# DeltaNet's Z·V, output and log-decay products from f16 pieces, and attention's exponentials directly behind the transposes

## The chip, the cores and the metric

The kernel runs on 1 core of one Trainium2 chip. The metric is the time of one execution in device microseconds. Five engines work side by side, each through its own program in order: TensorE (PE), VectorE (DVE), ScalarE (ACT), GpSimd (POOL) and SyncE (SP, which here issues loads). They wait for each other on semaphores.

## The reference

One layer of a hybrid encoder over 1024 positions of width 1024: four branches (GLA, RG-LRU, differential attention, DeltaNet) with a gated merge, cross attention over 256 memory positions, and a mixture of 32 experts. The change touches two branches. DeltaNet, in both directions, over chunks of positions:

```python
gam = jnp.cumsum(gc, axis=-1)
decay = jnp.exp(jnp.where(incl, gam[..., :, None] - gam[..., None, :], -jnp.inf))
a_mat = jnp.where(strict, bc[..., None] * kk * decay, 0.0) + jnp.eye(c)
sol = triangular_solve(a_mat, [vc * bc, kc * (bc * jnp.exp(gam))])   # u_val, k_cum
qk = jnp.einsum('bhntd,bhnsd->bhnts', qc, kc) * decay
q_dec = qc * jnp.exp(gam)[..., None]
def step(state, inp):
    v_new = u_i - kc_i @ state
    o = qd_i @ state + qk_i @ v_new
    state = cd_i * state + kd_i.T @ v_new
```

Differential attention, per head and block of 128 queries, with two maps m of 1024 keys each:

```python
s = jnp.einsum('bhmqd,bhmkd->bhmqk', q_blk, kt) + bias[None, :, None]
p = jax.nn.softmax(s, axis=-1)
attn = p[:, :, 0] - lam * p[:, :, 1]
return jnp.einsum('bhqk,bhkd->bhqd', attn, vt)
```

## The kernel before

One list of steps, `plan_schedule`, sets the order of the work up to the experts. Each engine goes through the same list and emits its own part of every step. `dense(..., between=...)` deals out the weight-streaming projections in pieces: a `None` in the list of a branch stands for one such piece (on PE often six f16 products of 512 columns; on ACT and DVE now and then the high and low halves of a weight chunk, L1346 and L1930, or the emptying of a PSUM bank, L1367, L1954 and L1960). For four panels POOL makes the low halves (L2692, L2694). So PE's long f16 projections are woven between the steps of attention and of DeltaNet, and fill its waits.

**Attention** (`diff_*`, 32 units u = head and query block; PE lines 885 to 921). Per unit: `diff_qk` (4 f16 products of 512 columns, L898; DVE adds the bias and takes the minimum, twice, L2249), `diff_exp` (two exponentials of 128x1024 on ACT, L1628), `diff_comb` (DVE: a reciprocal L2259, a factor L2261, the combination of the two maps L2264), `diff_tr` (8 f32 transposes, L911; ACT and DVE empty them as f16 high and low halves, L1637 and L2272), `diff_pv` (24 f16 products of 64 columns, L920; ACT L1644). In the list the unit's transposes are followed by one `None`, then the next unit's exponentials, another `None`, its combination, and this unit's `diff_pv`.

**DeltaNet's first half** (`gdn_a`) makes for each of the eight chunks of 128 positions, in both directions, the decayed matrices L and Q (`NLT`, `NQT`) and writes them to DRAM; the 32x32 diagonal blocks are inverted on DVE (`gdn_inv`, L2361 and L2364, many small rows), the second set of them during the first three chunks of the second half.

**The second half** (`gdn_c`, chunks i = 0 to 7, each for direction d = 0 and 1) has seven parts. A `None` stands behind parts 1 to 5, none behind parts 0 and 6.

- Part 0: POOL spreads the inverted blocks into `NX` and `NZ_` (L2764, 128x512 each, four per chunk) and copies the log decays (`NWK`, L2777), all behind the last chunk's value product. PE makes the sums of log decays (`gbc`, L1006: per direction 2 f32 products of 128 columns) and the first product Y of the block inverse (L1015); ACT the exponential of the sums (`NQD`, L1717).
- Parts 1 to 3: the block inverse Z grows from 32 to 64 to 128 (L1024, L1030, L1015; DVE L2381, L2384, L2385; ACT L1723, L1727).
- Part 4: PE multiplies keys with Z (L1037), ACT empties it (`wk`, L1731), DVE scales Q (L2388).
- Part 5: PE multiplies Z with V (L1043, 4 f32 products of 64 columns per direction, weights `NZ_`, right side `NVT`) and adds wk times the state (L1051); DVE makes V_new (`NVN`, `vn`, L2391).
- Part 6, per direction: PE makes the state's update (L1057), Q times state (L1062) and adds the output product (L1065, 4 f32 products of 64 columns, `NQT` times `NVN`). DVE masks the update (L2396), waits for the output product, and updates the state (L2401, two of 128x128, each with two SBUF operands); from chunk 4 on it adds the output to the other direction's (L2404), before that ACT copies it (L1735).

What an f32 matmul of the program is appears as two instructions in the trace.

The waits around the output product, in PE's part 6 and DVE's:

```python
pe.wait_ge(*v.at("qd", i, d))
...
mm.then_inc(*q.mark("o", i, d))
...
dve.wait_ge(*q.at("o", i, d))
for t in range(2):
    V.scalar_tensor_tensor(NS[d][:, t, :], NS[d][:, t, :], CD[:, d, c, t:t + 1], NKE[d][:, t, :], ALU.mult, ALU.add)
```

## Time and profile before

| | |
|---|---|
| median of 3 runs | 2118.31 us (2117.89 to 2120.36) |
| the profiled execution | 2124.99 us, span of its instructions 2123.2 us |
| PE busy | 1948.5 us (92%), weight loads 1171.6 |
| DVE busy | 1400.9 us (66%) |
| ACT busy | 1096.6 us (52%) |
| POOL busy | 294.1 us (14%) |
| mean granted TensorE clock | 0.96 of full speed |
| HBM | 307.85 MB read, 46.66 MB written |

Busy time counts an engine's instructions on the span from the first to the last. A matmul's own duration contains its way through the array and overlaps with the next one's, so the cost of a group is the distance from its start to the start of the next group. In a row, `[1.13 <-DVE arena L2264]` says that the engine sat idle for 1.13 us before it and was released by DVE's line 2264. `PE` is the matmul, `PEld` the load of its left matrix.

### The profile page before, as it was taken

The page shows a single profiled execution, that of the slowest core. Times are in us where ns is not written, and L with a number is a line of the kernel's source. Part 1 is how long each engine was busy: PE and PEld are TensorE (multiplying, and loading weights), DVE is VectorE, ACT ScalarE, POOL GpSimd, SP SyncE. Part 2 cuts the span into 40 slices and gives each one's busy share as a digit, 9 for nine tenths or more (in the row PEclk, how much of TensorE's full clock was granted, in tenths as well). Part 3 has the DMA queues.
Part 4 walks back from the last instruction along what each step waited for, and adds up shares of the span by engine and source line. Part 5 has one row for each costly group of instructions (what it writes and reads, how often), then busy time and mean ns, then how long its engine had stood idle before and what let it go on. Part 6 is the DMA issues. An engine that isn't in the chain of part 4 may idle for free. (4 is left out here: it accounts for less than half of the span.)

```text
span 2123.2 us, 32456 instructions
## 1 busy us (share of the span) xinstructions
PE 1948.5 (92%) x12820; PEld 1171.6 (55%) x12820; DVE 1400.9 (66%) x1794; ACT 1096.6 (52%) x1590; POOL 294.1 (14%) x276
## 2 busy tenths in 40 slices
PE   5999999899999999999989999898599999999991
PEld 3454566455544546787458865587345444444440
DVE  5555533788855696544442655435789999999985
ACT  3572232666646432212332444334478888888872
POOL 1000200343300613331000000000110111111103
PEclk8999999899999999999999999999699999999996
DMA  5411112112011342321511330311799999999976
GB/s 190 146 53 43 26 40 71 44 48 59 21 37 46 126 162 82 105 70 60 185 55 51 115 99 25 136 56 62 266 351 424 422 422 422 422 422 422 422 321 257
DMA packets 140520, 360.42 MB, mean 170 GB/s; under 512 B 38224, under 2 KB 91632, under 8 KB 113776
## 3 DMA queue, kind: packets, MB, share of 16 engines
q1 hardware_dynamic: 96608, 279.57, 34.9%
q10 hardware_dynamic: 34944, 46.14, 6.2%
q0 software_dynamic: 8848, 33.03, 4.0%
q8 instruction: 85, 1.39, 0.3%
q14 instruction: 35, 0.29, 0.0%
HBM read 307.85 MB, written 46.66 MB: 167 GB/s over the span
## 5 line engine op out<-in xcount | busy, mean ns | idle before, releaser
L780 PE MATMUL psum<-arena 128*128 128x512 f16 (+2 forms) x6000 | 1020.5, 328 | 12.9 <-ACT arena L1367 5.5
L780 PEld LDWEIGHTS psum<-arena 128*128 128x128 f16 x6000 | 571.4, 99 | 400.7 <-issue 30.9
L1184 PE MATMUL psum<-arena 128*128 128x512 f16 x2304 | 515.3, 383 | 15.5 <-issue 12.4
L739 DVE SCALAR_TENSOR_TENSOR arena<-arena 128x2048 f16<-128x2048 f32 x192 | 437.3, 2286 | 60.4 <-ACT arena L733 60.1
L733 ACT ACTIVATE arena<-arena 128x2048 f16<-128x2048 f32 x192 | 365.3, 1908 | 71.1 <-DMA arena<-in_w_dram 42.5
L1184 PEld LDWEIGHTS psum<-arena 128*128 128x128 f16 x2304 | 225.3, 99 | 283.5 <-issue 26.8
L1930 DVE SCALAR_TENSOR_TENSOR arena<-arena 128x512 f16<-128x512 f32 (+1 forms) x193 | 130.0, 694 | 129.5 <-ACT arena L1346 129.1
L2804 POOL DMA_INDIRECT arena<-xhat,arena x32 | 67.2, 2100 | 855.3 <-PE psum L1173 452.0
L1346 ACT ACTIVATE arena<-arena 128x512 f16<-128x512 f32 (+1 forms) x212 | 127.0, 616 | 27.1 <-DMA arena<-in_xattn_wo_dram 5.8
L1367 ACT ACTIVATE arena<-psum,arena 128x512 f32<-128x512 f32 x64 | 43.9, 685 | 160.5 <-PE psum L780 155.0
L1431 ACT ACTIVATE arena<-psum 128x512 f32<-128x512 f32 (+3 forms) x51 | 29.9, 586 | 126.1 <-PE psum L780 126.1
L1954 DVE SCALAR_TENSOR_TENSOR arena<-arena,psum 128x512 f32<-128x512 f32 x64 | 43.8, 684 | 61.3 <-PE psum L780 40.7
L1395 ACT ACTIVATE arena<-arena 128x256 f32<-128x256 f32 x64 | 26.7, 417 | 106.8 <-DVE arena L1966 105.8
L2249 DVE CUSTOM_DVE_ANT_0 arena<-psum,arena 128x1024 f32<-128x1024 f32 x64 | 75.6, 1219 | 0.6 <-PE psum L898 0.5
L1628 ACT ACTIVATE arena<-arena 128x1024 f32<-128x1024 f32 x64 | 72.9, 1145 | 4.5 <-DVE arena L2249 4.5
L1984 DVE SCALAR_TENSOR_TENSOR arena<-psum,arena 128x512 f16<-128x512 f32 x36 | 24.8, 690 | 68.0 <-ACT arena L1431 39.1
L1637 ACT ACTIVATE arena<-psum 128x512 f16<-128x512 f32 x64 | 34.8, 594 | 58.2 <-PE psum L911 36.8
L1966 DVE SCALAR_TENSOR_TENSOR arena<-psum,arena 128x512 f32<-128x512 f32 x32 | 22.1, 690 | 62.7 <-PE psum L780 62.7
L2764 POOL TENSOR_TENSOR arena<-arena 128x512 f32<-128x512 f32 x32 | 35.0, 1114 | 144.4 <-DMA arena<-gdn_inv 90.5
L2692 POOL TENSOR_SCALAR arena<-arena 128x512 f32<-128x512 f32 x19 | 36.5, 1920 | 132.0 <-ACT arena L1346 132.0
L797 PE MATMUL psum<-arena 128*128 128x128 f32 x144 | 23.0, 315 | 28.0 <-DVE arena L2054 28.0
L1845 ACT ACTIVATE arena<-psum 128x512 f32<-128x512 f32 x64 | 38.1, 597 | 12.7 <-PE psum L1184 12.4
(381 smaller groups left out, 2179.3 us busy)
## 6 DMA issues: line engine op xcount, KB each, us to landing
arena<-in_w_dram SPq DMA_DIRECT2D x192, 1024.0 KB, 11.9
arena<-in_merge_w_dram SPq DMA_DIRECT2D x64, 256.0 KB, 3.1
yrows<-arena ACTq DMA_DIRECT2D x32, 512.0 KB, 7.7
arena<-in_w_in_dram SPq DMA_DIRECT2D x48, 256.0 KB, 2.8
gdn_lq<-arena ACTq DMA_DIRECT2D x8, 1024.0 KB, 4.0
arena<-gdn_lq ACTq DMA_DIRECT2D x8, 1024.0 KB, 5.1
arena<-in_xattn_wkv_dram SPq DMA_DIRECT2D x32, 256.0 KB, 3.0
yrows<-arena POOLq DMA_DIRECT2D x1, 7680.0 KB, 24.2
```

The lines of the kernel that those rows point to most:

```text
L733: nc.scalar.activation(half_of(pieces(e, m)[0], half), half_of(XLAND[m], half), ACT.Copy, scale=WS).then_inc(w_hi[m], 1)
L739: nc.vector.scalar_tensor_tensor(half_of(lo, half), half_of(XLAND[m], half), WS, half_of(hi, half), ALU.mult, ALU.subtract).then_inc(w_lo[ ...
L780: mm = nc.tensor.matmul(bank[prt[0]:prt[1], c0:c1], lhs[a](k), rhs[b](k), start=(k == 0 and a + b == 0), stop=(k == nk - 1 and a == 1))
L1184: mm = nc.tensor.matmul(PS[:, bank, :], left[a][:, k, :], right[b][:, k, columns], start=k + a + b == 0, stop=(k == n - 1 and a == 1))
L1346: S.activation(W[i % 2][0][:, 2 * j:2 * j + 2, 0:wide], LAND[c % NLAND][:, :, 0:wide], ACT.Copy, scale=WS).then_inc(*act_hi.mark(c))
L1367: S.activation(SG[gate_no[n] % 2], bank, ACT.Tanh, scale=0.5 / WS, bias=half_b[:, 8 * kind[1] + kind[2]:8 * kind[1] + kind[2] + 1]).then_i ...
L1628: S.activation(DS[u % 2][:, m, :], DS[u % 2][:, m, :], ACT.Exp, scale=-1.0, bias=d_mx[u % 2][:, m:m + 1], accum_out=d_l[u % 2][:, m:m + 1])\
L1845: S.activation(YB[s][:, half, :], PS[:, 5 + half, :], ACT.Copy, scale=1 / (WS * GSCALE)).then_inc(act_y, 1)
L1930: V.scalar_tensor_tensor(W[i % 2][1][:, 2 * j:2 * j + 2, 0:wide], LAND[c % NLAND][:, :, 0:wide], WS, W[i % 2][0][:, 2 * j:2 * j + 2, 0:wid ...
L1954: V.scalar_tensor_tensor(dst, gate, 1.0, bank, ALU.add, ALU.mult).then_inc(*e.mark(n))
L2249: V.tensor_tensor_reduce(out=DS[u % 2][:, m, :], in0=PS[:, 2 + 2 * m:4 + 2 * m, :].rearrange("p a b -> p (a b)"), in1=DWH[:, 896 - P * qt: ...
L2804: G.indirect_dma_start(XR[e % 2], None, XH_D, bass.IndirectOffsetOnAxis(IDX[:, e:e + 1], 0)).then_inc(rows_in[e % 2], 16)
```

## The change

1. **Attention.** In the list of steps `diff_exp(u + 1)` moves ahead of the `None` that stood between it and the transposes.
2. **Z times V.** V is kept as two f16 pieces (`NVT16`: ACT writes the high one instead of `NVT`, DVE subtracts the low one, four operations of 128x512 each). Z gets two f16 pieces per direction and chunk: in part 3 ACT copies the high one (`z_hi`), DVE subtracts the low one (`z_lo`). The product becomes high·high, high·low and low·high: 12 f16 products instead of 4 f32 ones.
3. **The output product.** Q's pieces (`NQT16`, over `NY`) are made in part 4, the high one by ACT, the low one by POOL, behind its operations of part 1. V_new's pieces (`NVN16`, over `NWK`) are made by ACT in part 5 and by DVE at the head of each direction's part 6. Again 12 f16 products per direction instead of 4 f32 ones.
4. **The sums of log decays.** The log decays are scaled by 32 once, held from below at -60000 and split into two f16 pieces (3 small DVE operations in `gdn_gam`); POOL copies both for each direction and chunk (`NWK16`, over `NVN16`'s place), now behind all four spreads, and waits for the last chunk's output product. PE's sums (4 f16 products of 128 columns per direction) stand behind both directions' Y of part 0; ACT's exponential takes the scale back out.

The orders that result, as the builder lays them out. Lines of the changed kernel are shifted: L2396 became L2439 and L2401 became L2444, L2437 is V_new's low piece, L2426 Z's.

DVE in part 6 of chunk 3 and the head of part 0 of chunk 4, before:

```order
L2391 TENSOR_TENSOR arena<-psum,arena 128x256 x2
L2396 TENSOR_TENSOR arena<-psum,arena 128x256
L2401 SCALAR_TENSOR_TENSOR arena<-arena 128x128 x2
L2396 TENSOR_TENSOR arena<-psum,arena 128x256
L2401 SCALAR_TENSOR_TENSOR arena<-arena 128x128 x2
L2381 TENSOR_TENSOR arena<-psum,arena 128x512 x2
```

and now:

```order
L2432 TENSOR_TENSOR arena<-psum,arena 128x256 x2
L2437 TENSOR_TENSOR arena<-arena 128x256
L2439 TENSOR_TENSOR arena<-psum,arena 128x256
L2444 SCALAR_TENSOR_TENSOR arena<-arena 128x128 x2
L2437 TENSOR_TENSOR arena<-arena 128x256
L2439 TENSOR_TENSOR arena<-psum,arena 128x256
L2444 SCALAR_TENSOR_TENSOR arena<-arena 128x128 x2
L2419 TENSOR_TENSOR arena<-psum,arena 128x512 x2
```

A low piece stands ahead of each direction's masked update, the second one behind the first direction's state updates.

PE from part 6 of a chunk to part 1 of the next, before:

```order
L1057 MATMUL psum<-arena 128x128 x2
L1062 MATMUL psum<-arena 128x128 x2
L1065 MATMUL psum<-arena 128x64 x4
L1006 MATMUL psum<-arena 128x128 x2
L1015 MATMUL psum<-arena 128x128 x4
L1006 MATMUL psum<-arena 128x128 x2
L1015 MATMUL psum<-arena 128x128 x4
L1024 MATMUL psum<-arena 128x128 x4
```

and now (L1074 the output, L1019 is Y, L1083 the decay sums, L1028 the first product of part 1):

```order
L1063 MATMUL psum<-arena 128x128 x2
L1068 MATMUL psum<-arena 128x128 x2
L1074 MATMUL psum<-arena 128x64 x12
L1019 MATMUL psum<-arena 128x128 x8
L1083 MATMUL psum<-arena 128x128 x8
L1028 MATMUL psum<-arena 128x128 x4
```

The decay sums moved from ahead of each Y to behind both.

ACT in attention, before (L1637 empties transposes, L1346 is a weight chunk's high half, L1628 the exponentials):

```order
L1644 ACTIVATE arena<-psum,arena 128x64
L1637 ACTIVATE arena<-psum 128x512 x2
L1346 ACTIVATE arena<-arena 128x512
L1628 ACTIVATE arena<-arena 128x1024 x2
L1644 ACTIVATE arena<-psum,arena 128x64
```

and now, at the same place:

```order
L1660 ACTIVATE arena<-psum,arena 128x64
L1653 ACTIVATE arena<-psum 128x512 x2
L1644 ACTIVATE arena<-arena 128x1024 x2
L1362 ACTIVATE arena<-arena 128x512
L1660 ACTIVATE arena<-psum,arena 128x64
```

The weight copy moved behind the exponentials; this is so in 8 of the 31 units, and the others' order is as before.

The diff:

```diff
@@ plan_schedule
-        diff += [("diff_qk", u + 1)] * more + [("diff_tr", u, 0), ("diff_tr", u, 1), None] + [("diff_exp", u + 1)] * more
+        diff += [("diff_qk", u + 1)] * more + [("diff_tr", u, 0), ("diff_tr", u, 1)] + [("diff_exp", u + 1)] * more + [None]
@@ tiles
+        NVT16 = [f16(BR + 6144 + 1024 * x, TT, 256) for x in range(2)]
+        NZ16 = [[f16(UN + 2048 + 1536 * d + 256 * x, NH, P) for x in range(2)] for d in range(2)]
+        NQT16 = [[f16(UN + 2560 + 1536 * d + 256 * x, NH, P) for x in range(2)] for d in range(2)]
+        NVN16 = [[f16(UN + 5120 + 1280 * d + 512 + 128 * x, 2, P) for x in range(2)] for d in range(2)]
+        NWK16 = [[f16(UN + 5120 + 1280 * d + 512 + 128 * x, 2, P) for x in range(2)] for d in range(2)]
...
@@ PE, gdn_c
-                            pe.wait_ge(*po.at("lab", i, d))
-                            for t in range(2):
-                                mm = nc.tensor.matmul(B1[:, t, :], NWK[d][:, t, :], inc_b if d else inc_f, start=True, stop=True)
-                            mm.then_inc(*q.mark("gbc", i, d))
...
                         elif part == 5:
+                            pe.wait_ge(*v.at("z_lo", i, d))
                             for h in range(NH):
-                                nc.tensor.matmul(PS[:, 3 + 3 * d, h * 64:h * 64 + 64], NZ_[d][:, SLOT_OF[h], :],
-                                                 NVT[:, c, h * 64:h * 64 + 64], start=h == 0, stop=False)
+                                for x, y in ((0, 0), (0, 1), (1, 0)):
+                                    nc.tensor.matmul(PS[:, 3 + 3 * d, h * 64:h * 64 + 64], NZ16[d][x][:, SLOT_OF[h], :],
+                                                     NVT16[y][:, c, h * 64:h * 64 + 64], start=h + x + y == 0, stop=False)
...
+                            pe.wait_ge(*po.at("qt_lo", i, d))
+                            pe.wait_ge(*v.at("vn_lo", i, d))
                             for h in range(NH):
-                                mm = nc.tensor.matmul(PS[:, 2 + 3 * d, h * 64:h * 64 + 64], NQT[s][d][:, SLOT_OF[h], :],
-                                                      NVN[d].rearrange("p t n -> p (t n)")[:, h * 64:h * 64 + 64],
-                                                      start=False, stop=h == NH - 1)
+                                for x, y in ((0, 0), (0, 1), (1, 0)):
+                                    mm = nc.tensor.matmul(PS[:, 2 + 3 * d, h * 64:h * 64 + 64], NQT16[d][x][:, SLOT_OF[h], :],
+                                                          NVN16[d][y].rearrange("p t n -> p (t n)")[:, h * 64:h * 64 + 64],
+                                                          start=False, stop=h == NH - 1 and x == 1)
                             mm.then_inc(*q.mark("o", i, d))
+                    for d in range(2 if part == 0 else 0):
+                        B1 = PS[:, 3 + 3 * d, :].rearrange("p (h n) -> p h n", h=NH)
+                        pe.wait_ge(*po.at("lab", i, d))
+                        for t in range(2):
+                            for x in range(2):
+                                mm = nc.tensor.matmul(B1[:, t, :], NWK16[d][x][:, t, :], INC16[d], start=x == 0, stop=x == 1)
+                        mm.then_inc(*q.mark("gbc", i, d))
@@ ACT, gdn_c
+                        elif part == 5:
+                            act.wait_ge(*v.at("vn", i, d))
+                            S.activation(NVN16[d][0], NVN[d], ACT.Copy).then_inc(*a.mark("vn_hi", i, d))
...
+                    for d in range(2 if part in (3, 4) else 0):
+                        if part == 3:
+                            act.wait_ge(*a.at("z", i, d, 6))
+                            S.activation(NZ16[d][0], NZ_[d], ACT.Copy).then_inc(*a.mark("z_hi", i, d))
+                        else:
+                            act.wait_ge(lq_in[s], 48 * (i // 2) + 48)
+                            S.activation(NQT16[d][0], NQT[s][d], ACT.Copy).then_inc(*a.mark("qt_hi", i, d))
@@ DVE, gdn_c
+                        elif part == 3:
+                            dve.wait_ge(*a.at("z_hi", i, d))
+                            V.tensor_tensor(NZ16[d][1], NZ_[d], NZ16[d][0], ALU.subtract).then_inc(*v.mark("z_lo", i, d))
...
                         elif part == 6:
+                            dve.wait_ge(*a.at("vn_hi", i, d))
+                            V.tensor_tensor(NVN16[d][1], NVN[d], NVN16[d][0], ALU.subtract).then_inc(*v.mark("vn_lo", i, d))
                             dve.wait_ge(*q.at("u", i, d))
@@ POOL, gdn_c
                             spread(NX[d], d, d).then_inc(*po.mark("x", i, d))
                             spread(NZ_[d], 1 - d, d).then_inc(*po.mark("z", i, d))
+                        for d in range(2):
+                            if i:
+                                pool.wait_ge(*q.at("o", i - 1, d))
...
-                            G.tensor_copy(NWK[d].rearrange("p t (u n) -> p (t u) n", u=2), heads(LAd[:, d, c_, :]))\
-                                .then_inc(*po.mark("lab", i, d))
+                            for x in range(2):
+                                G.tensor_copy(NWK16[d][x].rearrange("p t (u n) -> p (t u) n", u=2), heads(LA16[x][:, d, c_, :]))\
+                                    .then_inc(*po.mark(*(("lab", i, d) if x else ("lab_hi", i, d))))
...
+                    elif part == 4:
+                        for d in range(2):
+                            pool.wait_ge(*counter("act_gdn").at("qt_hi", i, d))
+                            G.tensor_tensor(NQT16[d][1], NQT[s][d], NQT16[d][0], ALU.subtract).then_inc(*po.mark("qt_lo", i, d))
```

## Rows read from the trace of the kernel before

**Rows 1.** The page: busy time of each engine, and the longest chain by engine.

```profile
PE 1948.5 (92%) x12820; PEld 1171.6 (55%) x12820; DVE 1400.9 (66%) x1794; ACT 1096.6 (52%) x1590; POOL 294.1 (14%) x276
...
PE 25%; DVE 2%; DMA 1%; issue 1%; POOL 0%; ACT 0%; POOLq 0%; DVEq 0%
```

**Rows 2.** Stretches: length; PE, PEld, DVE, ACT, POOL busy; clock, DMA, GB/s.

```profile
372.00:600.00 228.00, 206.87 (x1710) 115.77 (x1709) 190.66 (x318) 145.49 (x272) 79.17 (x58) 0.97 0.15 40
...
809.00:995.00 186.00, 179.67 (x1532) 144.17 (x1531) 101.62 (x213) 39.14 (x91) 56.63 (x77) 1.00 0.25 73
```

**Rows 3.** Timeline, chunks 4 to 5: start us, duration, engine, line.

```profile
922.40 1.00 PE L1065 MATMUL psum<-arena 128*128 128x64 f32 x8
923.25 0.66 PE L1057 MATMUL psum<-arena 128*128 128x128 f32 x4
...
925.03 0.66 PE L1006 MATMUL psum<-arena 128*128 128x128 f32 x4
925.53 1.06 PE L1015 MATMUL psum<-arena 128*128 128x128 f32 x8
...
925.73 0.39 ACT L1717 ACTIVATE arena<-psum 128x256 f32<-128x256 f32 x1 [6.20 <-PE psum L1006]
```

**Rows 4.** Timeline of PE, attention: the f16 products of 64 columns.

```profile
479.81 0.87 PE L920 MATMUL psum<-arena 128*128 128x64 f16 x24 [0.41 <-DVE arena L2272]
480.52 1.03 PE L898 MATMUL psum<-arena 128*128 128x512 f16 x4
```

**Rows 5.** Timeline, attention: a unit whose weight copy precedes the exponentials.

```profile
439.92 0.63 ACT L1346 ACTIVATE arena<-arena 128x512 f16<-128x512 f32 x1
440.44 1.15 ACT L1628 ACTIVATE arena<-arena 128x1024 f32<-128x1024 f32 x1
...
444.76 1.09 PE L911 MATMUL psum<-arena 128*128 128x128 f32 x8 [1.13 <-DVE arena L2264]
```

**Rows 6.** Timeline, attention: another such unit, on PE.

```profile
423.74 1.03 PE L898 MATMUL psum<-arena 128*128 128x512 f16 x4
...
424.73 1.09 PE L911 MATMUL psum<-arena 128*128 128x128 f32 x8
```

**Rows 7.** Timeline, part 6 of chunk 6: POOL and DVE.

```profile
968.55 0.40 POOL L2777 COPY arena<-arena 128x256 f32<-128x256 f32 x1
968.70 0.66 PE L1057 MATMUL psum<-arena 128*128 128x128 f32 x4
968.91 2.09 POOL L2764 TENSOR_TENSOR arena<-arena 128x512 f32<-128x512 f32 x2
968.98 2.16 DVE L2401 SCALAR_TENSOR_TENSOR arena<-arena 128x128 f32<-128x128 f32 x2 [0.94 <-PE psum L1065]
```

**Rows 8.** Groups by shape, 809 to 995 us: busy us, mean ns; idle before.

```profile
L2764 POOL TENSOR_TENSOR arena<-arena 128x512 f32<-128x512 f32 x30 | 32.5, 1104 | 100.6 <-PE psum L1051 53.9 <-DMA arena<-gdn_inv 46.6
...
L1346 ACT ACTIVATE arena<-arena 128x512 f16<-128x512 f32 x9 | 5.6, 624 | 0.5 <-ACT arena L1367 0.5
...
L1960 DVE TENSOR_TENSOR arena<-arena 128x512 f32<-128x512 f32 x2 | 1.4, 692 | 0.1
```

**Rows 9.** Timeline, chunks 0 and 1.

```profile
822.90 0.38 ACT L1731 ACTIVATE arena<-psum 128x256 f32<-128x256 f32 x1 [1.56 <-PE psum L1037]
...
827.42 0.76 DVE L2391 TENSOR_TENSOR arena<-psum,arena 128x256 f32<-128x256 f32 x2
828.10 0.42 DVE L2361 TENSOR_TENSOR arena<-arena 128x210 f32<-128x210 f32 x1
...
830.18 1.11 DVE L2364 TENSOR_TENSOR arena<-arena 128x220 f32<-128x220 f32 x1
...
831.96 0.66 PE L1006 MATMUL psum<-arena 128*128 128x128 f32 x4
...
832.72 0.61 DVE L2401 SCALAR_TENSOR_TENSOR arena<-arena 128x128 f32<-128x128 f32 x2
...
853.69 0.71 PE L1057 MATMUL psum<-arena 128*128 128x128 f32 x4 [2.12 <-DVE arena L2391]
```

More of the change, by code:

```diff
@@ L434, in build @@
         LRUP = scol(256)
+        INC16 = [LRUP[:, 64 * d:64 * d + 64].bitcast(F16) for d in range(2)]
         g_em, g_ee, g_eem, g_mid, g_end = (scol(TT) for _ in range(5))
@@ L488, in build @@
         n_las, n_bes = n_t[2], n_t[3]
+        NVT16 = [f16(BR + 6144 + 1024 * x, TT, 256) for x in range(2)]
+        NZ16 = [[f16(UN + 2048 + 1536 * d + 256 * x, NH, P) for x in range(2)] for d in range(2)]
+        NQT16 = [[f16(UN + 2560 + 1536 * d + 256 * x, NH, P) for x in range(2)] for d in range(2)]
+        NVN16 = [[f16(UN + 5120 + 1280 * d + 512 + 128 * x, 2, P) for x in range(2)] for d in range(2)]
+        LA_SCALE = 32.0
+        LA16 = [n_t[1].bitcast(F16)[:, 64 * x:64 * x + 64].rearrange("p (d c h) -> p d c h", d=2, c=TT) for x in range(2)]
+        NWK16 = [[f16(UN + 5120 + 1280 * d + 512 + 128 * x, 2, P) for x in range(2)] for d in range(2)]
         LAS = n_las.rearrange("p (d c h) -> p d c h", d=2, c=TT)
@@ L1709, in _ @@
                     i, part = step[1:]
+                    s = i % 2
                     a, v, q = (counter(f"{e}_gdn") for e in ("act", "vec", "pe"))
@@ L2297, in _ @@
                         V.tensor_tensor(dst, dst, NSQ, ALU.mult).then_inc(*v.mark("norm", s))
+                elif step == ("gdn_tm", "nv"):
+                    v, a = counter("vec_gdnp"), counter("act_gdnp")
+                    for j in range(4):
+                        dve.wait_ge(*a.at("tm", "nv", j))
+                        V.tensor_tensor(NVT16[1][:, 2 * j:2 * j + 2, :], PS[:, 2 + j, :].rearrange("p (c n) -> p c n", c=2),
+                                        NVT16[0][:, 2 * j:2 * j + 2, :], ALU.subtract).then_inc(*v.mark("tm_lo", j))
                 elif what == "gdn_scal":
@@ L2326, in _ @@
                                 .then_inc(*v.mark("slots", by_slot is n_bes, u))
+                    V.tensor_scalar(n_tmp[:, 0:64], n_la, LA_SCALE, -60000.0, ALU.mult, ALU.max).then_inc(*v.mark("la_scaled"))
+                    dve.wait_ge(*v.last())
+                    V.tensor_copy(n_t[1].bitcast(F16)[:, 0:64], n_tmp[:, 0:64]).then_inc(*v.mark("la_hi"))
+                    dve.wait_ge(*v.last())
+                    V.tensor_tensor(n_t[1].bitcast(F16)[:, 64:128], n_tmp[:, 0:64], n_t[1].bitcast(F16)[:, 0:64], ALU.subtract).then_inc(*v.mark("la_lo"))
                     for par in range(2):
@@ L2788, in _ @@
                                 .then_inc(*po.mark("kd", i, d))
+                    elif part == 4:
+                        for d in range(2):
+                            pool.wait_ge(*counter("act_gdn").at("qt_hi", i, d))
+                            G.tensor_tensor(NQT16[d][1], NQT[s][d], NQT16[d][0], ALU.subtract).then_inc(*po.mark("qt_lo", i, d))
                 elif what == "experts_first":
```

7 lines of the change are left out of this document (4 added, 3 removed).

## The prediction

> **What bounds the kernel now.** I read the page's busy times and its longest chain first: TensorE (PE) is busy for 1948.5 us of the 2123.2, and the last stretch of the program belongs to PE too, in lines that the change leaves alone [rows 1]. So what counts is how long PE needs for the two stages that are edited, and I read those by the table of stretches [rows 2]. In attention (372 to 600 us) PE is busy for 206.9 of 228 us and VectorE (DVE) for 190.7: two engines that take turns in waiting for each other. In DeltaNet's second half, the eight `gdn_c` chunks from 809 to 995 us, PE is busy for 179.7 of 186 us. Only 6.3 us of PE stalls are left there, DVE has 84 us free, GpSimd (POOL) 129. PE's program is in order and nothing after 995 us starts by a clock of its own, so a microsecond won or lost by PE in either stage is one at the end.
>
> **What PE saves in a chunk.** The cost of a group of matmuls is the distance between the starts of neighbouring groups. The four f32 products of the output in one direction take 923.25 - 922.40 = 0.85 us, the four of Z and V, of the same shape and number, as much; the two sums of log decays 925.53 - 925.03 = 0.50 and, behind other f32 groups, 0.45 [rows 3]. Their f16 form has three products for one, of 64 columns each. Attention has exactly this form: 24 of them take 480.52 - 479.81 = 0.71 us, 0.030 each [rows 4]. So twelve take 0.36. A 128-column f16 product is taken as two of these, so the four of a decay sum take 0.23. Saved in both directions: 0.98 + 0.98 + 0.49 = 2.45 us in a chunk, 19.6 us in eight.
>
> This rests on a row of f32. The Trainium skill says otherwise: FP8 and Floating Point Precision, section TensorE Precision Notes, has a true f32 product as four passes through the array. With 64 columns at 2.4 GHz that is an estimate of 0.107 us for a product, not 0.21, and the sum of savings would be some 5 us instead of 19.6; the group of four in the trace contradicts it.
>
> **What the chunk pays for that.** The pieces are made by three engines, and where they stand in each queue decides.
>
> 1. *Decay sums.* They now stand behind both Y products of part 0, and behind them comes a product that waits for ACT's exponential. Both Y groups take 1.78, the sums 0.46. The first exponential can start 0.20 behind its sum and takes 0.39 [rows 3], plus 0.1 to wake PE: PE, ready at 2.24 us of the chunk, starts at 2.70. This is a new stall of 0.45 us, 3.6 in all; the start of the chunk is as late as before, and the sums' saving is nearly all given back.
>
> 2. *Z's pieces.* Two ACT copies of 0.62 and two DVE subtractions of 0.69 (a 128x512 tile on either engine) [rows 8] lie between part 3 and part 5, where PE has two dense pieces and the wk products, some 3.7 us of cover. I cost them at nothing in quiet chunks; DVE is not quiet in chunks 0 and 1 (below). The DVE halves of `NVT16` (four of 0.69) follow ACT's copies one by one before DeltaNet's first stage, where POOL's first product is awaited anyway: nothing. The three small operations on log decays: nothing, they are needed 90 us later.
>
> 3. *Q's pieces.* ACT copies 128x512 twice behind its wk copies, POOL subtracts twice, 1.10 each by its spreads of the same size [rows 8]. In a chunk let V be the moment at which the first direction's value product ends. POOL's second subtraction ends about V+1.25, and only then do its four spreads of the next chunk run, 1.04 each, to V+5.4. Before, they began at V+0.25.
>
> 4. *The output product of the second direction.* This is the place that decides. On DVE the order is now: low piece of V_new, masked update, the two state updates, for one direction and then for the other. The state update waits for that direction's output product. So the second low piece stands behind the first direction's output, and PE's second output behind that low piece. PE ends output 0 at V+3.4 and could start output 1 at V+4.35. DVE begins the state updates 0.28 later than output 0 ended, as in the trace (968.70 to 968.98). Undisturbed they take 0.61 for two, and the low piece about 0.4, half of the 0.76 of two such tiles [rows 9]: ready at V+4.8, a stall of 0.5, and 0.9 in chunks 4 to 7, where DVE's addition of `NO` (0.41) stands between. This is the lower bound.
> But POOL is not idle then. At 968.91 POOL runs two spreads, and DVE's two state updates, which read two SBUF tiles each, take 2.16 us instead of 0.61 [rows 7, 9]: each waited for one POOL operation to end. With POOL busy to V+5.4, then with the two decay copies of 0.40, the updates end at V+5.6, the low piece at V+6.25: a stall of 2.0, and 2.35 in chunks 4 to 6. I take the upper values, since the spreads cover exactly this stretch by the rows.
>
> 5. *The output of the first direction.* Its low piece of V_new is in time unless a weight chunk's low half (L1930) stands ahead of it: chunks 2 and 4. There both meet POOL's spreads, and I count 1.3 more for each.
>
> 6. *Chunks 0 and 1.* Here DVE also works on the second block inverse (L2361, L2364: small operations on two SBUF tiles). One of them took 1.11 with POOL at work, about 0.43 alone. Before, V_new was made at 827.42 and output 1 ended at 831.96, where the next chunk's first group starts. ACT's two wk copies of 0.38 began at 822.90; they begin 0.5 earlier now, and Q's first copy of 0.62 ends behind them at 823.8 [rows 8, 9]. DVE's own work on two tiles lets POOL begin with Q's low pieces at about 824.15. POOL then runs six operations, with one DVE operation let in after each, every 1.15 us: to 831.05. DVE's last two rows, V_new and six more rows end at 835.3, and only then comes the low piece, at 835.7. PE's output 0 ends at 836.2, output 1 at 838.15: chunk 0 ends 6.2 us later, its savings included. In chunk 1 V_new was late already, and PE waited 2.12 for it at 853.69. Z's subtractions (1.4), Q's (each holds DVE up by about 0.7) and the products of V_new behind them make it 2.5 later still.
>
> Chunk by chunk, savings (2.0 with the stall of point 1) against stalls: +6.2, +2.5, +1.3, 0.0, +1.7, +0.4, -0.5 (it had 0.9 of stall before), and -1.1 in the last, which has no spreads behind it. **The stage: +10.5 us.**
>
> **Attention.** The exponentials move ahead of one dense piece. PE's and DVE's orders don't change; on ACT a weight copy (L1346) stood between transposes and exponentials in 8 of 31 units and now stands behind. It held up the exponential by 440.44 - 439.92 = 0.52 us. PE then waited 1.13 for DVE's combination, which waits for the exponential [rows 5]: three units are like this, and each gives back the 0.52, some more with the next wait. In four the scores of the next unit start at 423.74 and the transposes at 424.73, only 0.13 more than those scores take [rows 6]: 0.13 each. The eighth gives nothing. 1.6 + 0.5, rounded up for the waits behind: **-2.5 us.** POOL's halves of these weights come 2.3 us later and aren't due before the panel's last quarter.
>
> **Sum.** +10.5 - 2.5 = +8.0 us on the profiled execution, whose own time is 2124.99 (span 2123.2). The median of the runs shown is 2118.3, 6.7 lower; I add the same change to it: 2126.3.
>
> **Rivals.** About 0.2%, 4.2 us, is what a measurement of this kernel can tell from no change.
> - *The savings win.* If POOL's spreads don't coincide with the state updates, point 4 costs its lower bound, 4 x 0.5 + 4 x 0.9 = 5.6; chunk 0 keeps only the six rows ahead of the low piece, 3 more; of 19.6 - 3.6 = 16.0 us remain 7.4, with attention 9.9: 2108.4. For it: POOL has 129 us free, and some state updates in the trace took 0.61. Against it: Q's subtractions push the spreads later, onto the updates.
> - *A wash.* Half of the contention: the stage ends midway between +10.5 and -7.4, at +1.5, attention at -2.5: 2117.3.
> - *Attention turns slower.* One mechanism: POOL's scaling of the moved weight copy becomes ready within 0.1 us of DVE's combination. If POOL starts first, DVE waits up to the length of that operation, some 1.4 us, in seven units, 0.85 net each: +6 in place of -2.5, so 2134.8. It decides from a delay of 0.1 us in DVE.
> - *The f16 products are no faster behind f32 groups.* Then nothing is saved and the stalls stay: 2126.3 + 19.6 = 2145.9. Against it: [rows 4] is the same form, with a new left matrix for each product too.
>
> **Chances.** Forecast (2120 to 2133) 0.48; the savings win 0.22; a wash 0.18; attention slower 0.09; no saving 0.03. The range, short of the far ends: 2108 to 2135, from the savings' win to attention's loss. Faster by over 0.2%: 0.23; within: 0.22; slower: 0.55.
>
> **What would show it.** Right: PE waits before the output product, released by DVE's low piece, about 2 us in most chunks, and before the Z·X product by ACT's exponential, 0.45; state updates of 1.1 us each; stage 809 to 995 about 196 us; attention about 225.5. Wrong: PE stalls before the output of 0.5 to 0.9 with state updates of 0.36 us, or chunk 0 no longer than before; then the stage is under 180 us and the kernel faster.

## The result, and the profile after

The changed kernel takes 2142.23 us (median of 4 runs, 2139.90 to 2142.92) against 2118.10 before (4 runs): a ratio of 1.0111, 95% interval 1.0098 to 1.0123. The forecast was 2126.3, with 2135 as its upper end. The direction was right, the size three times too small.

The page's busy times, where [rows 1] stood before:

```profile
PE 1938.2 (91%) x12948; PEld 1162.4 (54%) x12948; DVE 1435.2 (67%) x1833; ACT 1118.2 (52%) x1638; POOL 328.8 (15%) x310
```

TensorE (PE) works 10 us less in a longer execution. The stretches that answer to [rows 2], attention and DeltaNet's second half (length; PE, PEld, DVE, ACT, POOL busy; clock, DMA, GB/s):

```profile
372.00:600.00 228.00, 208.97 (x1736) 118.19 (x1735) 192.06 (x326) 149.66 (x280) 87.85 (x62) 0.98 0.16 43
802.00:1014.10 212.10, 176.24 (x1651) 136.40 (x1650) 132.53 (x242) 61.40 (x139) 83.04 (x109) 0.91 0.22 64
```

The second half takes 212.0 us (802.11 to 1014.07), 184.7 before (809.36 to 994.04): +27.3. The clock column fell from 1.00 to 0.91. Chunk by chunk, from the first product of a chunk (before the decay sums L1006, now Y, L1019) to that of the next:

| chunk | 0 | 1 | 2 | 3 | 4 | 5 | 6 | 7 | sum |
|---|---|---|---|---|---|---|---|---|---|
| before, us | 22.60 | 25.35 | 23.51 | 22.11 | 22.10 | 22.38 | 24.17 | 22.46 | 184.7 |
| after | 29.75 | 30.23 | 31.19 | 22.46 | 23.49 | 26.62 | 25.28 | 22.94 | 212.0 |
| difference | +7.2 | +4.9 | +7.7 | +0.4 | +1.4 | +4.2 | +1.1 | +0.5 | +27.3 |
| forecast | +6.2 | +2.5 | +1.3 | 0.0 | +1.7 | +0.4 | -0.5 | -1.1 | +10.5 |
| PE waits, before | 0.3 | 2.7 | 1.3 | 0.0 | 0.0 | 0.0 | 0.9 | 0.9 | 6.1 |
| PE waits, after | 6.8 | 7.5 | 8.0 | 2.2 | 2.8 | 3.4 | 3.7 | 1.1 | 35.5 |

PE's waits in this stage (us in total, times, longest; L1063 is the state's update, L1074 the output product, L1041 keys times Z, L1028 the first product of part 1; L2432 makes V_new, L2437 its low piece):

```profile
PE psum L1063 <- DVE arena L2432: 18.6, 3, 7.2
PE psum L1074 <- DVE arena L2437: 11.7, 8, 2.7
PE psum L1041 <- ACT arena L1744: 2.1, 2, 1.2
PE psum L1028 <- DVE arena L2419: 2.0, 6, 0.3
```

Chunk 1, in order of time. L2426 is Z's low piece, L1987 and L1957 belong to the woven projections, L2429 scales Q, L2399 and L2402 are rows of the second block inverse, L2841 Q's low piece, L2809 the spreads:

```profile
845.25 1.29 DVE L2426 TENSOR_TENSOR arena<-arena 128x512 f16<-128x512 f32 x2 [0.24 <-ACT arena L1759]
...
846.95 2.72 POOL L2841 TENSOR_TENSOR arena<-arena 128x512 f16<-128x512 f32 x2 [11.70 <-ACT arena L1762]
...
847.18 1.47 DVE L1987 TENSOR_TENSOR arena<-arena 128x512 f32<-128x512 f32 x1
...
848.42 1.46 PE L788 MATMUL psum<-arena 128*128 128x512 f16 x6
848.57 2.55 DVE L2429 TENSOR_TENSOR arena<-arena 128x256 f32<-128x256 f32 x2
849.62 4.99 POOL L2809 TENSOR_TENSOR arena<-arena 128x512 f32<-128x512 f32 x4
851.05 1.52 DVE L1957 SCALAR_TENSOR_TENSOR arena<-arena 128x512 f16<-128x512 f32 x1
852.49 1.23 DVE L2399 TENSOR_TENSOR arena<-arena 128x228 f32<-128x228 f32 x1
...
853.75 1.12 DVE L2402 TENSOR_TENSOR arena<-arena 128x228 f32<-128x228 f32 x1
...
856.57 0.76 DVE L2432 TENSOR_TENSOR arena<-psum,arena 128x256 f32<-128x256 f32 x2
...
857.05 1.23 PE L1063 MATMUL psum<-arena 128*128 128x128 f32 x4 [7.17 <-DVE arena L2432]
...
858.92 0.85 PE L1074 MATMUL psum<-arena 128*128 128x64 f16 x12
```

From 846.95 to 854.61 GpSimd (POOL) works without a pause, and each VectorE (DVE) operation on two SBUF tiles takes about as long as one of POOL's: L2429 2.55 for two instead of 0.75, L2399 1.23 where one after 854.61 takes 0.39. The value products end at 848.4, PE has one dense piece, and V_new is made at 856.57. The Trainium skill has this rule (SBUF — State Buffer, section Who interferes with whom): a DVE instruction with two SBUF inputs contends with a GpSimd instruction that reads SBUF. The durations above agree.

What follows the wait is the part that the forecast lacks. PE's update of the state (L1063) takes 1.23 where it took 0.71 behind a wait in [rows 9], and the output's twelve products reach from 858.92 to 859.58, where the next group starts: 0.66 instead of the 0.35 of chunk 3. The clock over the same time:

```profile
848.00:852.00 4.00, 1.88 (x12) 0.90 (x10) 4.00 (x4) 0.00 (x0) 4.00 (x5) 1.00 0.01 1
852.00:856.00 4.00, 0.00 (x0) 0.00 (x0) 3.86 (x6) 0.00 (x0) 2.62 (x3) 0.55 0.25 66
856.00:860.00 4.00, 2.95 (x22) 2.89 (x23) 2.22 (x7) 0.94 (x3) 0.17 (x1) 0.50 0.02 4
860.00:862.00 2.00, 2.00 (x19) 1.94 (x19) 1.44 (x4) 0.19 (x1) 0.63 (x2) 0.50 0.00 0
862.00:864.00 2.00, 2.00 (x21) 2.00 (x19) 1.37 (x3) 0.38 (x1) 1.66 (x4) 0.84 0.00 0
864.00:866.00 2.00, 1.66 (x19) 1.50 (x18) 0.91 (x2) 0.66 (x2) 1.46 (x3) 1.00 0.00 0
```

It fell to 0.50, its 1.2 GHz level, while PE waited, and came back at 863. In slices of 2 us over the stage, PE's busy time times (1 - clock) comes to 13.7 us; this is called lost pace here. It lies behind the waits of chunks 0, 1 and 2, and again at 937 to 945, 965 to 969 and 992 to 996. Before, the same sum is 0.0. The stage alone, before and now:

```profile
809.36:994.04 184.68, 178.35 (x1522) 143.08 (x1521) 100.93 (x210) 39.14 (x91) 56.27 (x77) 1.00 0.25 74
```

```profile
802.11:1014.07 211.96, 176.10 (x1650) 136.28 (x1649) 132.53 (x242) 61.40 (x139) 82.93 (x109) 0.91 0.22 64
```

PE's busy time without its lost pace fell from 178.35 to 176.10 - 13.7 = 162.4, by 16.0. So the sum closes: 29.4 us more of waiting and 13.7 of lost pace, less 16.0 saved, are +27.1, of +27.3 measured.

### The profile page after: what moved, and what is told of

Read it like the earlier page. It is cut to its first block and busy times, and to the rows that moved or that the text cites. A ratio compares the mean times of both kernels' runs of the same rounds, so it can differ in the third digit from the quotient of the medians.

```text
span 2140.3 us, 32849 instructions
## 1 busy us (share of the span) xinstructions
PE 1938.2 (91%) x12948; PEld 1162.4 (54%) x12948; DVE 1435.2 (67%) x1833; ACT 1118.2 (52%) x1638; POOL 328.8 (15%) x310
## 5 line engine op out<-in xcount | busy, mean ns | idle before, releaser
L1957 DVE SCALAR_TENSOR_TENSOR arena<-arena 128x512 f16<-128x512 f32 (+1 forms) x193 | 131.0, 700 | 115.0 <-ACT arena L1362 114.7
L2735 POOL TENSOR_SCALAR arena<-arena 128x512 f32<-128x512 f32 x19 | 44.7, 2352 | 133.8 <-ACT arena L1362 133.8
L805 PE MATMUL psum<-arena 128*128 128x128 f32 x144 | 23.2, 316 | 28.4 <-DVE arena L2081 28.4
L919 PE MATMUL psum<-arena 128*128 128x128 f32 x256 | 35.0, 281 | 9.9 <-DVE arena L2291 9.8
```

Source lines behind the costliest of these rows:

```text
L1957: V.scalar_tensor_tensor(W[i % 2][1][:, 2 * j:2 * j + 2, 0:wide], LAND[c % NLAND][:, :, 0:wide], WS, W[i % 2][0][:, 2 * j:2 * j + 2, 0:wid ...
L2735: G.tensor_scalar(landed_c, landed_c, WS, None, ALU.mult).then_inc(*counter("pool_w_scaled").mark(c))
```

## The experiments

Ratios are to the kernel before, run on the same chip, with 95% intervals.

**1. Attention alone.** Edit: the kernel before with the list's line of the change.

> The kernel before with the attention edit alone. The recorded theory gives it 2.5 us: 2115.6 us against 2118.1, a ratio of 0.9988. The rival reads the trace of the changed kernel, in which DeltaNet's second half begins at 802.1 us instead of 809.4: if all of that comes from the edit, 2111 us, a ratio of 0.9965, and attention (372 to 600 us) has its last value product near 580 us instead of 584.5.

Measured: 2113.89 against 2116.61 us, 0.9991 (0.9978 to 1.0004). The interval holds 1, so the times alone show no gain; the traces do. Attention's value products run from 391.6 to 584.3 us, from 392.3 to 587.9 before: 2.9 us shorter; and in all traces of this case they span 192.7 to 193.1 us with the edit and 195.6 to 196.6 without it. The forecast's 2.5 holds. Of the 7.3 us by which the changed kernel's trace was ahead at 802, 2.6 lie there, 2.0 ahead of attention and 2.7 behind it. The latter two are no effect of the edit: the stretch behind attention took 221.5 us before and 218.4 in experiment 12, by the same code.

**2. DeltaNet alone.** Edit: the changed kernel with the list's old line.

> The changed kernel with attention's old order, so the DeltaNet edits alone. DeltaNet's second half took 212.0 us in the changed kernel and 184.7 before. If this whole difference is its own, the time is 2118.1 + 27.3 = 2145.4 us (ratio 1.0129), and the sum with the attention edit gives the changed kernel back. Rival: the second half's length depends on where attention leaves the other engines, and then the stage is shorter than 205 us here.

Measured: 2144.76 us, 1.0133 (1.0116 to 1.0150), the stage 210.4 us. The loss is the DeltaNet edits' own.

**3. Q's low pieces on DVE.**

```diff
-                            G.tensor_tensor(NQT16[d][1], NQT[s][d], NQT16[d][0], ALU.subtract).then_inc(*po.mark("qt_lo", i, d))
+                        V.tensor_tensor(NQT16[d][1], NQT[i % 2][d], NQT16[d][0], ALU.subtract).then_inc(*v.mark("qt_lo", i, d))
```

> The changed kernel with Q's low pieces on VectorE (behind its scaling of Q in part 4) instead of GpSimd. Theory: GpSimd's two subtractions and the four spreads pushed behind them are what VectorE's inverse rows wait for in chunks 0 to 2; TensorE's waits for V_new fall from 18.6 us to 6 or less, its clock no longer halves there, the output product's waits fall from 11.7 to about 5: 2116 to 2122 us. Rival: the spreads meet the rows wherever they start, as they did before, and VectorE has 1.4 us more to do in each chunk: the waits for V_new stay above 12 us and the time above 2134.

Measured: 2138.79 us, 1.0104 (1.0088 to 1.0121). PE's waits:

```profile
PE psum L1063 <- DVE arena L2432: 17.4, 4, 6.8
PE psum L1074 <- DVE arena L2437: 10.3, 8, 2.4
```

The rival was right. In chunk 1 DVE now carries the subtractions itself, 2.97 us for two since the spreads begin with them, at 848.42, and V_new's wait there is 6.8 instead of 7.2 us.

**4. Without the inverse's rows.** Edit: the loop over the rows of the second block is left out, its last three operations stay; so the second block isn't inverted.

> The changed kernel without the rows of the second block inverse (that part of the computation is left out). Theory: the excess of chunks 0 to 2 (7.1 + 4.9 + 7.7 us against before) is these rows meeting GpSimd, with the halved clock that follows; it goes, less 1 us: 2142.2 - 18.7 = 2123.5 us, no wait for V_new over 1 us, and the clock halves in chunks 4 to 6 alone. Rival: V_new is late since its pieces and Z's stand ahead of it on VectorE and ScalarE; then waits for V_new stay, and the time is above 2136.

Measured: 2128.66 us, 1.0050 (1.0034 to 1.0067); the stage 196.2 us instead of 212.0. Chunk 0 is at 22.7, chunk 1 at 25.1, as before the change; chunk 2 is at 27.6, where it was 23.5 before. The time lies between theory and rival: the rows account for 13.6 us by the medians, not for all 18.7. PE still waits 4.6 us for V_new and 14.2 for its low pieces.

**5. Z times V alone.** Edit: the kernel before with part 2 of the change only.

> The kernel before with Z times V from f16 pieces alone: no pieces of Q or V_new, decay sums as before, attention as before. A group of twelve f16 products stands 0.35 us from the next one in the changed kernel's trace, four f32 ones 0.85, so TensorE saves 16 x 0.5 = 8.0 us. Theory: VectorE's two more subtractions (1.3 us) delay V_new in chunks 0 to 2 only, by some 1.3 us each where it was already late: 2118.1 - 8.0 + 4 = 2114, stage about 180.5 us (184.7 before), the clock at full level throughout. Rival: these subtractions alone push V_new behind GpSimd's spreads and bring the waits of 5 to 7 us and the halved clock: above 2130.

Measured: 2125.82 us, 1.0029 (1.0015 to 1.0043), between theory and rival; the stage takes 193.3 us, 6.8 of them lost pace. PE's waits for V_new:

```profile
PE psum L1061 <- DVE arena L2407: 11.0, 3, 5.5
```

Chunks 3 to 7 are 21.2 to 22.9 us long, 0.3 to 1.3 less each than before: there the pieces of Z are hidden and the products' saving arrives. In chunk 1, V_new is 5.5 us late instead of 2.1: by an estimate from both traces 1.3 for Z's low pieces, 1.0 since PE gets there sooner, 0.9 since one more DVE operation falls under the spreads. So neither Q's pieces nor V_new's are needed for the long wait.

**6. The rows dealt out otherwise.**

```diff
-            if i < 3 and part in (1, 2, 4) or (i, part) == (0, 5):
+            if i < 3 and part in (1, 2, 3) or (i, part) == (3, 0):
```

> The changed kernel with the second block inverse's rows dealt out otherwise: behind parts 1, 2 and 3 of chunks 0 to 2 and part 0 of chunk 3, instead of parts 1, 2 and 4 and once part 5. So none of them stands between V_new's operands and V_new. Theory: the waits for V_new (18.6 us) fall under 4 us, since rows meet GpSimd's subtractions and spreads only where they stand in part 4; the halved clock of chunks 0 to 2 (9.5 us of lost pace) goes with them: 2142.2 - 15 - 9 = 2118 us. Rival: VectorE has too much work in these chunks wherever it stands: 2132 or more.

Measured: 2138.45 us, 1.0083 (1.0060 to 1.0106), waits for V_new 16.5 us. The theory fell, by a fault of the edit's: a row behind part 3 still stands ahead of V_new in DVE's queue. In chunk 1 five of these six operations took 1.12 to 1.36 us under POOL's work.

**7. V_new's low pieces in part 5.**

```diff
-                            V.tensor_tensor(NVN16[d][1], NVN[d], NVN16[d][0], ALU.subtract).then_inc(*v.mark("vn_lo", i, d))
+                    for d in range(2 if part == 5 else 0):
+                        dve.wait_ge(*a.at("vn_hi", i, d))
+                        V.tensor_tensor(NVN16[d][1], NVN[d], NVN16[d][0], ALU.subtract).then_inc(*v.mark("vn_lo", i, d))
```

> The changed kernel with V_new's two low pieces on VectorE in part 5, directly behind V_new, instead of at the head of each direction's part 6; nothing else is moved. Theory: TensorE's waits for the low pieces (11.7 us in 8) fall to 3 or less, and the halved clock in chunks 4 to 6 (some 5 us of lost pace) goes: 2142.2 - 8.7 - 5 = 2128.5 us, chunks 0 to 2 unchanged. Rival: the state updates behind GpSimd's spreads hold TensorE anyway, through the masked update or the next chunk's value product: less than 4 us gained, above 2138.

Measured: 2132.84 us, 1.0059 (1.0042 to 1.0076), 9.4 us better than the change and 4.3 short of the theory. The 11.7 us of waits for low pieces are gone; 6.4 came back ahead of the next chunk's Y (L1019), for DVE's addition of `NO` behind the state updates (L2445):

```profile
PE psum L1063 <- DVE arena L2432: 18.5, 3, 7.2
PE psum L1019 <- DVE arena L2445: 6.4, 6, 2.1
```

**8. Both.**

> The last two edits together: rows dealt out otherwise and V_new's low pieces in part 5. If the two waits and the clock behind them are the whole loss, the gains add up: 2118 - 13.7 = 2104 us, faster than the kernel before by 0.6%, stage about 173 us. Rival: one wait takes the other's place: 2115 or more.

Measured: 2129.80 us, 1.0047 (1.0034 to 1.0060). The rival's time was right, its reason in part: V_new's waits, 16.5 us, had not gone at all, and `NO`'s addition brings 6.4 as in experiment 7.

**9. The inverse begun earlier, low pieces in part 5.** Edit: the second set of diagonal blocks is read behind the first inverse, twelve rows stand ahead of chunk 0, none behind parts 3 and 4.

> The changed kernel with V_new's low pieces in part 5 and the second block inverse begun earlier: its diagonal blocks are read right behind the first inverse, its first twelve rows stand in the dense pieces ahead of chunk 0, the others behind parts 1 and 2 of chunks 0 to 2, none behind part 4. Theory: with rows out of the stretch in which GpSimd works, V_new is in time; against the kernel with both edits (2129.8) its waits for V_new of 16.5 us fall under 3 and 5.6 us of lost pace go with them: 2129.8 - 13.5 - 5 = 2111 us. Rival: VectorE is behind in these chunks for another reason than rows: above 2122.

Measured: 2122.10 us, 1.0019 (1.0009 to 1.0029), at the rival's bound. But the rows were the reason for most of it: V_new's waits fell from 16.5 to 4.6 us. PE waited 2.6 us ahead of the stage, and ran at half the clock there too: the diagonal blocks landed late (DVE waits 3.13 us for them, to 795.41), and the rows met POOL's first spreads at 798.15.

**10. The same rows, with Z times V and attention alone.**

> The kernel before with Z times V from f16 pieces, the attention edit, and the second block inverse begun earlier as in the last kernel. From the run with Z times V alone (2125.8): its waits for V_new were 11.0 us and its lost pace 6.8; without them 2108, with attention's 2 us 2106: faster than before by 0.5%. Rival: rows behind parts 1 and 2 hold Z's low piece and the waits move there: 2116 or more.

Measured: 2113.66 us, 0.9972 (0.9962 to 0.9983), between theory and rival. Within the stage the clock stays full. Ahead of it PE waited 2.9 us, and the clock halved there too.

**11 and 12. A wait by itself.** Edit: the kernel before, with 10 or 5 idle operations ahead of V_new in chunks 4 to 7.

```diff
+                            if i >= 4 and d == 0:
+                                dve.wait_ge(inv_out[1], 32)
+                                for k in range(10):
+                                    V.tensor_scalar(NU[1], NU[1], 1.0, None, ALU.mult).then_inc(*v.mark("delay", i, k))
+                                    dve.wait_ge(*v.last())
```

> The kernel before with ten idle operations of some 0.7 us on VectorE ahead of the first direction's V_new in chunks 4 to 7 (no part of the change). TensorE stalls some 5.4 us in each. Theory: after such a stall the granted clock halves for 5 to 6 us, as in chunks 0 to 2 of the changed kernel, and each costs some 3 us beyond its stall: 2118 + 4 x 8.4 = 2152. Rival: the halved clock belongs to the f16 products or to the time at which they run, not to a stall: 2118 + 21.6 = 2140, clock at full level between 809 and 1015.

> The same with five such operations: TensorE stalls 1.8 us in each of the four chunks. If the halving needs a long stall, as chunk 3 of the changed kernel (1.9 us, no halving) lets one think, 2118 + 7 = 2125 and full clock; if stalls of this size are enough, as after 1.8 + 0.65 us in its chunk 4, up to 2118 + 7 + 12 = 2137.

Measured: 2160.19 us, 1.0196 (1.0179 to 1.0213), and 2138.87, 1.0095 (1.0077 to 1.0113). The waits came out longer than expected, the cost behind them as the first theory has it. With ten, PE waits 8.2, 8.2, 8.2 and 5.2 us, and the four chunks are 39.9 us longer; 10.2 of that is no waiting. Chunk 4, by the table of stretches:

```profile
922.00:930.00 8.00, 0.87 (x4) 0.87 (x5) 7.76 (x10) 0.00 (x0) 3.88 (x4) 0.60 0.00 0
930.00:934.00 4.00, 4.00 (x21) 4.00 (x21) 1.52 (x6) 0.00 (x0) 0.39 (x1) 0.51 0.21 66
936.00:938.00 2.00, 2.00 (x21) 2.00 (x20) 0.98 (x3) 0.47 (x2) 1.15 (x2) 1.00 0.00 0
```

With five, waits of 3.7, 3.7 and 3.0 us are each followed by the halved clock, one of 1.5 is not; what 1.8 us in each chunk would do, the waits being twice that, these chunks don't tell. The program around them is the kernel before: the halving needs no f16 product and no pieces. Chunk 1, which holds no idle operation, shows more (the last line is from the table of stretches):

```profile
850.82 1.22 PE L1057 MATMUL psum<-arena 128*128 128x128 f32 x4 [2.12 <-DVE arena L2396]
...
852.68 1.81 PE L1065 MATMUL psum<-arena 128*128 128x64 f32 x8
...
852.00:856.00 4.00, 4.00 (x21) 4.00 (x20) 1.46 (x4) 0.38 (x1) 0.70 (x2) 0.50 0.02 4
```

It is the wait of 2.12 us of [rows 9]. There L1057 took 0.71 behind it; here 1.22, and the chunk 28.6 us instead of 25.35, with 2.7 us of waits in both. So this short wait cost its length in three executions and 3 us more in a fourth. The Trainium skill says that an idle gap can lower PE's clock, so that the next work starts at half (TensorE: Matmul & The Clock Gate, section HAM oscillation — how this bites in real kernels); these runs agree.

**13 to 15. Control and the two better versions.** Edit of all three; 14 adds Z times V and attention, 15 is the whole change with V_new's low pieces in part 5:

```diff
+        ... + [("gdn_read", 1)] * (p == 8)
-    gdn += [("gdn_back", 0)] + [None] * 6 + [("gdn_load_inv", 0), ("gdn_load_inv", 1), ("gdn_read", 1)] + [None] * 7
+    gdn += [("gdn_back", 0)] + inv(1, 0) + [None] * 2 + inv(1, 1) + [None] * 2 + inv(1, 2) + [None] * 2
+    gdn += [("gdn_load_inv", 0), ("gdn_load_inv", 1)] + [None] * 7
-            if i < 3 and part in (1, 2, 4) or (i, part) == (0, 5):
-                gdn += inv(1, 3 * i + (i > 0) + (1, 2, 4, 5).index(part))
+            if i < 3 and part in (1, 2):
+                gdn += inv(1, 2 * i + part + 2) + inv(1, 9) * ((i, part) == (2, 2))
```

> The kernel before with nothing but the second block inverse begun earlier (nine rows ahead of chunk 0, none behind part 4). It is the control for the next two. Before, V_new was late by 2.1 us in chunk 1, with 0.6 behind it: theory, that goes and nothing else: 2118.7 - 2.7 = 2116, ratio 0.9987. Rival: its rows ahead of chunk 0 meet GpSimd's first spreads, and it is 2120 or more.

> As the kernel with Z times V, the attention edit and the inverse begun earlier (2113.7), but the diagonal blocks are read before the first inverse is ready, so that the rows ahead of chunk 0 run from 792 to 799 us and not from 799 to 813. There TensorE waited 2.9 us ahead of the stage and ran at half the clock for 2 to 4 us. Theory: 5 us less, 2108.5, ratio to before 0.995. If the Z-times-V pieces win nothing beyond the control, it is the control's time less attention's 2 us: 2114.

> The whole change with V_new's low pieces in part 5 and the inverse begun earlier in the same way. From its predecessor (2122.1), whose trace shows 2.6 us of wait ahead of the stage and 4.5 us of lost pace within: 2115, ratio 0.998. If the whole change is sound and only its place was wrong, it beats the control; if the f16 output product doesn't pay for its pieces, it stays behind the kernel with Z times V alone by 5 us or more.

Measured:

| | us | ratio to before | stage, us | clock |
|---|---|---|---|---|
| 13, rows moved alone | 2114.05 | 0.9975 (0.9964 to 0.9987) | 181.3 | 1.00 |
| 14, with Z times V and attention | 2107.85 | 0.9962 (0.9947 to 0.9976) | 175.5 | 1.00 |
| 15, the whole change | 2114.95 | 0.9983 (0.9972 to 0.9994) | 186.3 | 0.97 |

The stage's row in 13, 14 and 15:

```profile
807.50:988.80 181.30, 177.80 (x1522) 143.09 (x1522) 92.14 (x192) 39.15 (x91) 53.87 (x76) 1.00 0.25 75
```

```profile
804.50:980.10 175.60, 171.14 (x1587) 134.83 (x1586) 104.87 (x208) 47.59 (x107) 55.10 (x76) 1.00 0.26 78
```

```profile
805.40:991.80 186.40, 168.23 (x1650) 128.58 (x1650) 124.50 (x224) 61.60 (x139) 84.13 (x108) 0.97 0.24 73
```

Kernel 14 has the lowest median of all, and beats both kernels of this case. Chunk 1 in it:

```profile
840.18 1.29 DVE L2402 TENSOR_TENSOR arena<-arena 128x512 f16<-128x512 f32 x2 [0.36 <-ACT arena L1743]
...
841.95 0.69 PE L1056 MATMUL psum<-arena 128*128 128x128 f32 x4
...
843.36 2.60 POOL L2781 TENSOR_TENSOR arena<-arena 128x512 f32<-128x512 f32 x2 [14.23 <-DMA arena<-gdn_inv]
843.38 0.69 DVE L1938 SCALAR_TENSOR_TENSOR arena<-arena 128x512 f16<-128x512 f32 x1
843.99 0.75 DVE L2408 TENSOR_TENSOR arena<-psum,arena 128x256 f32<-128x256 f32 x2
...
844.64 0.61 PE L1062 MATMUL psum<-arena 128*128 128x128 f32 x4
```

V_new (L2408) is made at 843.99, with nothing but a weight's low half (L1938) between it and the spreads' start at 843.36; PE goes on at 844.64 with no wait. The control tells how much of it is due to the rows alone: 4.3 us by the medians, with 3.4 us off the stage. Z times V takes 5.8 us more off the stage; the medians of 13 and 14 are 6.2 apart, which holds the attention edit's 2 to 3 us too.

Kernel 15 beats the kernel before, but not by the change: the control, with the rows alone, is as fast (2114.05 by 2114.95, though 15 has the attention edit as well). Its stage is 10.8 us longer than 14's, and 5.0 longer than the control's. What it waits for (L1020 is Y, L1064 the state's update, L1029 part 1; L2446 adds `NO`, L2433 makes V_new, L2420 masks Y):

```profile
PE psum L1020 <- DVE arena L2446: 6.4, 6, 2.1
PE psum L1064 <- DVE arena L2433: 4.9, 3, 3.1
PE psum L1029 <- DVE arena L2420: 2.6, 4, 1.5
```

PE is busy for 2.9 us less than in 14, and 4.7 of its busy time is lost pace; its waits are 17.6 us, 4.2 in 14. So the f16 output product and decay sums together cost more than their faster matmuls give, with the pieces where 15 makes them. The two were not run apart, so what each of them costs is not shown.

## Why the prediction was right or wrong

Forecast: +8.0 us. Measured: +24.1. By the prediction's own steps:

- **What PE saves in a chunk** (2.45 us). Twelve f16 products: 912.38 - 912.03 = 0.35 against the 0.36 taken; right, and the four-pass estimate of 0.107 us for an f32 product stays contradicted. The eight products of the decay sums start 0.056 apart at full clock, 0.45 in all against 0.46; both Y take 1.87, not 1.78. By distances of starts that is 2.4 a chunk, some 19.3 in all against 19.6. PE's busy time fell by only 16.0. An estimate of why: where a wait follows, the last product's way through the array is no longer covered by the next one and counts as busy, as in the 0.61 us that the row of the sums lasts.
- **Point 1**, a new wait of 0.45 behind the sums: 0.34, in six chunks. Right. The view names DVE's L2419 as the releaser; but the mask that this product needs was done at 895.18 in chunk 3, and ACT's exponential at 895.99, 0.15 before PE went on, as forecast.
- **Point 2**, Z's pieces for nothing: right in chunks 3 to 7, wrong before (experiment 5).
- **Points 3 and 4.** Chunk 3 went nearly as written, with V, the end of the first value product, at 908.97:

```profile
907.93 2.42 POOL L2841 TENSOR_TENSOR arena<-arena 128x512 f16<-128x512 f32 x2 [11.27 <-ACT arena L1762]
...
910.30 4.26 POOL L2809 TENSOR_TENSOR arena<-arena 128x512 f32<-128x512 f32 x4
...
911.14 0.61 PE L1063 MATMUL psum<-arena 128*128 128x128 f32 x4
...
912.65 2.06 DVE L2444 SCALAR_TENSOR_TENSOR arena<-arena 128x128 f32<-128x128 f32 x2 [0.44 <-PE psum L1074]
...
914.63 0.61 DVE L2437 TENSOR_TENSOR arena<-arena 128x256 f16<-128x256 f32 x1
...
915.39 0.51 PE L1074 MATMUL psum<-arena 128*128 128x64 f16 x12 [1.88 <-DVE arena L2437]
```

  The spreads run from V+1.3 to V+5.6 (forecast 1.25 and 5.4), the state updates take 2.06 for two (forecast 2.16), and PE waits 1.88 before output 1 (2.0). Later chunks show 2.7 and 2.5 (2.35); 0.65 in chunk 4, where output 0 had taken the wait. Chunk 2 has none of this wait, since V_new came after the spreads there. Right but for that.
- **Point 5**, 1.3 us at output 0 in chunks 2 and 4: 1.82 in chunk 4, 0.38 in chunk 2, where V_new was the later one. Half right.
- **Point 6.** Right for chunks 0 and 1 in place and size: +7.2 and +4.9, which are +4.7 and +2.1 without the lost pace, against 6.2 and 2.5. It stopped one chunk too early. The last rows of the inverse stand behind part 4 of chunk 2 as well, with two operations of 1.03 and 0.69 us behind them:

```profile
885.38 1.03 DVE L2405 TENSOR_SCALAR arena<-arena 128x1024 f32<-128x1024 f32 x1
...
887.71 1.22 PE L1063 MATMUL psum<-arena 128*128 128x128 f32 x4 [6.06 <-DVE arena L2432]
```

  Six operations of the rows, of 0.93 to 1.20 us (0.2 alone), ran under POOL's, V_new came at 887.26, and PE waited 6.1. Forecast: +1.3, measured: +7.7, or +5.1 without the lost pace. This step failed.
- **"Savings against stalls"**, the sum itself. It priced a wait at its length. The forecast's waits were 30.1 us (10.5 + 19.6), the measured ones 29.4 more than before: that total was right, partly by errors that cancel. The 13.7 us of lost pace behind them had no term: the clock stood at 1.00 in this stage before [rows 2], and the forecast took it to stay there. They make most of the 16 us that were missing. This is the step that decided, and experiments 11 and 12 show it on a kernel without the change.
- **Attention**, -2.5: 2.9 us in the trace, 2.7 by the medians. Right. The three units with the long wait gave 0.61 to 0.64 each (forecast 0.52). The four others gave 0.26 each, twice the forecast: a wait of 0.40 ahead of their value products went, and 0.32 of the gain came back in the next unit. In no trace with the edit is attention slower, as the rival would have it.

Left open: how much of V_new's lateness is POOL's doing and how much DVE's own load. Taking Q's pieces from POOL gave it to DVE (experiment 3); experiment 5, which has them on neither, still waits 11.0 us for V_new instead of 18.6, but it lacks V_new's pieces as well.

## What to carry to other kernels

An engine's wait in the middle of dense TensorE work can cost more than its length: behind every wait of 3 us and more in DeltaNet's second half, in all traces, the clock halved, and each such wait brought 1.5 to 3.4 us of lost pace. So a stage with hardly a wait has more to lose than its trace shows, and edits that trade PE time for waits need that term. Before adding work to an engine, list everything in its queue ahead of the value that PE waits for, in every repetition of the stage, special ones included; here background rows that could as well have run earlier, and the place of one subtraction, decided between +1.1% and -0.2%, and the rows alone, without the change, gave the same -0.2%. And split a change that has several parts: here Z times V paid once the rows had moved, and the f16 output product with the decay sums cost more than it gave.

## What the runs showed of the hardware

- The clock's fall behind a short wait isn't the same in every execution: 2.1 us, preceded by no other in that chunk but 0.6, left it full in three traces and halved it in one, with 3.3 us on the chunk. Over DeltaNet's second half in all traces of this case, eleven waits of PE are 2.07 to 2.14 us long, and behind six of them the clock halved; thirty are 2.96 us or longer, and it halved behind or within each. The 2.5 us wait at the end of chunk 6 was followed by the fall in the changed kernel's trace, and not in that of experiment 2, whose DeltaNet is the same.
- It can fall and come back late enough to hit work that had nothing to wait for: behind chunks 4 and 5 (939 to 945 and 966 to 969 us) it was the next chunk's Y products that ran at half.
- What stands between POOL's large operations counts for DVE. Before, a log-decay copy of 0.55 us stood between the two pairs of spreads, and the DVE operation beside it took 0.45 in chunk 1, the ones beside the spreads 1.10 to 1.15. Now six operations of 128x512 stand in one row, 7.66 us long, and the DVE operations on two SBUF tiles beside them take 1.12 to 1.52 us each.
